# The input projection's step-size products, and VectorE's sums of them, one modulation group later

## What is computed

```python
mod = jax.nn.silu(c) @ lw['w_ada'] + lw['b_ada']
sh1, sc1, g1, sh2, sc2, g2 = jnp.split(mod[:, None, :], 6, axis=-1)
h = rmsnorm(x, lw['g_pre_mix']) * (1 + sc1) + sh1
# in the mixer:
proj = h @ lw['w_in']
z, xbc, dt_raw, q, k, v = jnp.split(proj, [o1, o2, o3, o4, o5], axis=-1)
dt = jax.nn.softplus(dt_raw.astype(jnp.float32) + lw['dt_bias'].astype(jnp.float32))
```

## Time and profile before

| | us |
|---|---|
| median of 3 runs | 1894.21 |
| lowest and highest run | 1889.01, 1897.79 |
| span of the profiled execution, first to last instruction | 1892.2 |
| TensorE busy in it | 1722.1 (91%) |
| VectorE busy | 1004.1 (53%) |
| ScalarE busy | 663.9 (35%) |
| mean rate of all transfers | 206 GB/s |

### The profile page before, as it was taken

How to read it: one execution, slowest core, us unless ns; L and a number is a source line. 1 busy time by engine, 2 the same in 40 slices (tenths; PEclk the granted TensorE clock), 3 DMA queues, 4 the chain that set the end, 5 groups by cost and what they waited for, 6 DMA issues and landing times.

```text
span 1892.2 us, 32067 instructions
## 1 busy us (share of the span) xinstructions
PE 1722.1 (91%) x13926; PEld 1549.3 (82%) x13926; DVE 1004.1 (53%) x1281; ACT 663.9 (35%) x655; POOL 53.5 (3%) x151
## 2 busy tenths in 40 slices
PE   5888998998777988988976999999999999999997
PEld 3767877886556655667965999999999999999996
DVE  2434454454657424435547655646656556565666
ACT  3333122222743433214245433333333333333344
POOL 3000000001000000000000000000000000000000
PEclk9989998999888985689987999999999999999999
DMA  9778796988368983246871544545445454454541
GB/s 340 250 245 289 245 321 246 323 311 313 105 216 315 389 328 106 78 155 226 282 249 49 174 156 159 175 157 169 166 158 176 157 166 169 157 175 159 164 149 68
DMA packets 183077, 389.51 MB, mean 206 GB/s; under 512 B 7635, under 2 KB 16067, under 8 KB 182641
## 3 DMA queue, kind: packets, MB, share of 16 engines
q1 hardware_dynamic: 179488, 375.68, 57.3%
q0 software_dynamic: 2752, 9.24, 1.4%
q10 hardware_dynamic: 698, 2.55, 0.4%
HBM read 377.03 MB, written 10.41 MB: 205 GB/s over the span
## 4 chain that ended last, share of the span: by engine, by line
PE 80%; DVE 7%; DMA 5%; ACT 4%; issue 2%; SPq 2%; DVEq 0%; ACTq 0%
PE ps L780 14%; PE ps L779 14%; PE ps L778 14%; PE ps L759 7%; PE ps L760 6%; PE ps L761 6%; PE ps L739 4%; PE ps L700 4%; PE ps L960 1%; SPq L449 1%; DMA kring<-in_cache_k_dram 1%; DVE wlo L1696 1%; PE ps L1097 1%; DMA raw<-in_w_in_dram 1%; PE ps L711 1%
## 5 line engine op out<-in xcount | busy, mean ns | idle before, releaser
L1696 DVE TENSOR_TENSOR wlo<-raw,whi 128x2048 fp32r<-128x2048 f32 x146 | 332.9, 2287 | 205.6 <-ACT whi L1359 204.0
L1359 ACT ACTIVATE whi<-raw 128x2048 fp32r<-128x2048 f32 x145 | 277.6, 1916 | 449.8 <-PE ps L780 372.5
L778 PE MATMUL ps<-h2hi,whi 128*128 128x288 f32 x1408 | 417.0, 296 | 9.5 <-DVE h2lo L1765 8.7
L780 PE MATMUL ps<-h2hi,wlo 128*128 128x288 f32 x1408 | 419.8, 298 | 0.0
L779 PE MATMUL ps<-h2lo,whi 128*128 128x288 f32 x1408 | 416.8, 296 | 0.0
L778 PEld LDWEIGHTS ps<-h2hi,whi 128*128 128x128 f32 x1408 | 265.5, 189 | 10.5 <-DVE h2lo L1765 9.5
L779 PEld LDWEIGHTS ps<-h2lo,whi 128*128 128x128 f32 x1408 | 266.4, 189 | 0.0
L780 PEld LDWEIGHTS ps<-h2hi,wlo 128*128 128x128 f32 x1408 | 265.1, 188 | 0.0
L759 PE MATMUL ps<-hhi,whi_in 128*128 128x288 f32 x704 | 209.6, 298 | 7.1 <-DVE wlo L1696 7.1
L760 PE MATMUL ps<-hlo,whi_in 128*128 128x288 f32 x704 | 209.2, 297 | 0.0
L761 PE MATMUL ps<-hhi,wlo 128*128 128x288 f32 x704 | 209.0, 297 | 0.0
(11 more groups left out here) (423 smaller groups left out, 2367.8 us busy)
## 6 DMA issues: line engine op xcount, KB each, us to landing
raw<-in_w_ffn_in_dram SPq DMA_DIRECT2D x88, 1024.0 KB, 5.0
raw<-in_w_ada_dram SPq DMA_DIRECT2D x84, 1024.0 KB, 8.4
raw<-in_w_in_dram SPq DMA_DIRECT2D x44, 1024.0 KB, 5.2
raw<-in_w_ffn_out_dram SPq DMA_DIRECT2D x44, 1024.0 KB, 5.0
kring<-in_cache_k_dram SPq DMA_DIRECT2D x64, 512.0 KB, 6.1
vring<-in_cache_v_dram SPq DMA_DIRECT2D x64, 512.0 KB, 5.8
raw<-in_w_out_dram SPq DMA_DIRECT2D x14, 1024.0 KB, 7.2
araw<-in_w_ada_dram SPq DMA_DIRECT2D x8, 1024.0 KB, 18.6
```

Of the source, the lines that this page charges most:

```text
L778: mm(o, high[:, q, cols], xh, start=(first and q == 0), stop=False)
L780: i = mm(o, low[:, q, cols], xh, start=False, stop=(last and q == QC - 1))
L1359: fn(high_of(g), landed_at(u), ACT.Copy).then_inc(hi_ready, 1)
L1696: tt(low_of(u), landed_at(u), high_of(g).bitcast(F32), SUB).then_inc(lo_ready, 1)
```

## The change

The groups in which the step-size products of quarters 1, 2 and 3 stand on TensorE, and their additions on VectorE, become those of the units 20, 28 and 44 in place of 16, 24 and 40. Quarter 0 stays at unit 8. Where the quarters are prepared (PREPARED) stays as it was, and so does the place within a group: ahead of j = 2 on TensorE, ahead of `rows_of` on VectorE. All waits stay in the text; the one for `mod_ready` counts the folds made so far, so it is for the sum of the group in which the products now stand.

```diff
     PREPARED = {16: 1, 24: 2, 40: 3}
+    STEPS = (8, 20, 28, 44)
@@ on TensorE, in ada()
-                if j == 2 and pos.ada - 2 in (8, *PREPARED):
+                if j == 2 and pos.ada - 2 in STEPS:
                     dt_products()
@@ on VectorE, in ada(a)
                 if j == 3:
-                    if a - 3 in (8, *PREPARED):
+                    if a - 3 in STEPS:
                         dt_part()
                     rows_of()
```

## The result

| | before | changed kernel |
|---|---|---|
| median of 4 runs, us | 1894.61 | 1867.51 (1857.53 to 1876.17) |
| ratio, 95% interval | | 0.9871 (0.9829 to 0.9914) |
| span of the profiled execution, us | 1892.2 | 1874.1 |
| first to last weight product of the projection, us | 388.3 | 368.2 |

The account below looks back on a forecast made before the run. TensorE, with work for 91% of the span, was taken to bound the kernel. Gains of 4.1, 7.75 and 9.5 us for quarters 1 to 3 sum to 21.3 us: 1894.2 - 21.3 = 1872.9 us, range 1864 to 1884 us.

Parts of the forecast that it names:

- The bound and what each wait cost: Input projection: TensorE bounds; three step-size groups take 13.2, 11.15 and 12.9 us extra; at most 31.5 us can go.
- The wait for hlo is met: Moved step-size products find the quarter's low part ready, after 13 to 19 us more work; 24.4 us of waits go.
- VectorE keeps up behind the prepared quarter: After groups 24 and 40, VectorE finishes before TensorE's weight products need it, with 2.5 and some 2 us of cover.
- The new wait, group 20: Quarter 1's step-size products wait 4.6 us for the modulation sum, the clock falls, product 11 starts at 154.9; 4.1 us gained.
- Groups 28 and 44: Quarters 2 and 3: 1.9 us work plus 1.25 to 1.65 us wait, about 3.4 us each; 7.75 and 9.5 us gained.
- Nothing gives it back: After the projection TensorE stays on the path, so later stages keep the whole gain of 21.3 us.
- (a): Clock falls at all three new waits, the short ones costing 2.35 us more: 16.6 us gained, 1877.6 us; chance 0.12.
- (b): Modulation sum comes early, group 20's wait is under 2 us and the clock holds: 27 us gained, 1867.2 us; chance 0.07.
- (c): Transfers become the bound, weights behind groups 24 or 40 late: about 10 us gained, 1884 us, or 1894 us; chance 0.12.
- (d): Slower: new waits lower the clock through weight products; at five low-clock products 1904.9 us; chance 0.03.

Follow-up runs that it names:

- the version that avoids all of it: Changed kernel with step-size products of quarters 1 to 3 ahead of weight products 13, 24 and 35, outside the groups; ratios to the kernel before 0.9829 and 0.9854.
- own bank: Changed kernel with step-size products written to a free PSUM bank of the next weight product instead of bank 6; ratio to the kernel before 0.9849.
- groups 36 and 52: Changed kernel with step-size products of quarters 2 and 3 in groups 36 and 52 instead of 28 and 44; ratio 0.9950.
- filled wait: Changed kernel with 16 extra matmuls, results not used, in TensorE's wait of group 20; ratio to the kernel before 0.9897.
- quarters 2 and 3 alone: Changed kernel with only quarters 2 and 3 moved, to groups 28 and 44; quarter 1 stays in group 16; ratio 0.9931.

## Why the prediction was right

**The bound and what each wait cost.** Right. Three waits of 24.4 us cost 31.5 us beyond the work; the version that avoids all of it gained 29.8 in the projection (30.9 between the second traces).

**The wait for hlo is met.** Right: no such wait in any kernel with the new places, and groups 16, 24 and 40 at 4.45 to 4.46 us.

**VectorE keeps up behind the prepared quarter.** Right: no weight product waited after groups 24 and 40. This cover was costed at 2.5 and 2 us, and nothing used it up: the low part of weight 16 was done at 188.2, 3.1 us ahead of its product.

**The new wait, group 20.** Forecast: the sum there at 148.8, a wait of 4.6 us, the low clock, product 11 at 154.9. Measured: 148.3, 4.58 us, the low clock, 154.89. That it agrees to 0.1 us is luck in part: over three traces the wait was 4.52 to 5.26 us, and two errors of mine offset each other. The work from the landing of the weight to the sum took 7.2 us where I had 7.7, and from the release to product 11 it was 6.4 us where I had 6.1; the whole trace lies 0.3 us earlier besides. Its causes are tested by a run each: the bank (own bank: no wait), the loads of a group after two products (groups 36 and 52: 5.21 and 4.89 us), the idle time behind the slow matmuls (filled wait: 2.6 us back; I had 2.35).

**Groups 28 and 44.** Forecast 3.4 us over an undisturbed group; measured 3.8 and 4.0, in the later traces 3.6 to 3.8. The mis-sized term is the wait, 1.25 to 1.65 forecast and 1.50 to 1.87 measured. The sums: 20.1 us against 21.3 in the projection. The difference is these two groups (1.0 us) and group 20 (13.79 for 13.5).

**Nothing gives it back.** Right in matched traces: 21.2 and 17.7 us of span for 19.6 and 19.2 us of projection. I had not seen that later stages move by 11 and 6 us from run to run by themselves. The range held because its ends lay 9 to 11 us from the forecast, not because it had a term for that. The measured ratios, 24 and 14 us, lie on both sides of the 20 us that the projection shows. Whether the shift of 20 us changes how often the later stages meet the low clock stays open; the traces are too few.

**The rivals.** (a) did not come in the changed kernel, but its mechanism is real: behind waits of 1.99 us (filled wait) and 2.41 us (quarters 2 and 3 alone) the clock fell in such a group, and from the release to the next product it was 5.4 us in place of 3.75. The rule that I cited beside it, from the Trainium skill (TensorE: Matmul & The Clock Gate, the section on psum-queue depth-cycling), speaks of frequent short idles; these two runs agree with it only in that a single short wait was followed by a fall, and the waits of up to 1.87 us in the three traces of the changed kernel were followed by none. (b) did not come: the first load to the fifth landing took 141.12 - 124.03 = 17.1 us in group 20, as before. (c) came as 0.4 to 0.6 us in group 36 in two of three traces, and as 1.5 us in the kernel with its own bank. (d) did not: the clock was back before or just at the next weight product. The chances hold a slip: the forecast, (a), (b) and half of (c) add up to 0.91, where I wrote 0.89.

## What to carry to other kernels

A step that has time until much later should not stand in an in-order queue ahead of work that doesn't need it; find the last place where its inputs are certain and its buffer still free, not merely the next group. When a step is moved, list every wait that it takes along: here the one that had always been met (a shared PSUM bank) became the longest at the new place, and its length could be forecast to within 0.7 us from the rows of a group of the same kind. Here every stall of TensorE of 4.5 us or more was paid again in slow matmuls behind it, and so were two of 1.99 and 2.41 us, so a gain is read from start to start across the whole group, not from the row of waits.

## What was not expected of the hardware

The clock fell after an idle wait of 1.99 and 2.41 us in two runs, when TensorE had already been at work again for 1.0 and 1.1 us, and stayed through the six waits of 1.50 to 1.87 us in the three traces of the changed kernel. In six long stalls it fell 3.1 to 4.1 us after the last matmul. Other things than the wait's length may decide between these, and the runs don't tell which.

The same 64 matmuls of one stage lie in a stretch at a granted clock of 0.57 in one trace of the kernel before and of 0.98 in the other, 28.7 against 17.5 us, with nothing changed in the kernel. No idle time shows beside the low clock: from 740 to 770 us the first trace has TensorE busy throughout and the clock at 0.50, the second has it busy for 27.0 of the 30 us and the clock at 1.00. And the feed-forward part ran at two rates with the clock shown as 1.00 in both. In the window from 1200 to 1300 us the kernel before and the changed kernel's first trace, each with TensorE busy for all 100 us and the clock at 1.00, ran 752 matmuls against 746, 0.8% apart; what sets the rate was not found.
